# Banded self-attention: the order of four value matmuls and the signal at their end

## The reference

```python
kb, vb = with_prev(kr), with_prev(vr)          # key and value block n-1 and n, side by side
scores = jnp.einsum('bnqhgd,bnkhd->bhgnqk', qb, kb).astype(jnp.float32) * (SWA_HEAD_DIM ** -0.5) + bias
scores = jnp.where(mask, scores, -jnp.inf)
...
probs = jax.nn.softmax(jnp.concatenate([scores, sink], axis=-1), axis=-1)[..., :-1]
out = jnp.einsum('bhgnqk,bnkhd->bnqhgd', probs.astype(v.dtype), vb)
```

## Time and profile before

| | us |
|---|---|
| median of 3 executions (2558.08 to 2558.94) | 2558.24 |
| span of the profiled execution, first to last instruction | 2555.1 |
| PE busy | 2131.7 |
| DVE busy | 1672.5 |
| ACT busy | 1296.7 |
| from the first transpose of unit 0 to the last PV of unit 15 | 126.7 |

### The profile page before, as it was taken

One profiled execution on the slowest core, in us unless ns is written; L12 is line 12 of the kernel. 1 busy time (PEld: TensorE's weight loads), 2 busy tenths in 40 slices (PEclk: granted clock), 3 DMA queues, 4 the chain that ended last, 5 costly groups with the idle time before them and its releaser, 6 DMA issues.

```text
span 2555.1 us, 27563 instructions
## 1 busy us (share of the span) xinstructions
PE 2131.7 (83%) x9450; PEld 1695.3 (66%) x9450; DVE 1672.5 (65%) x1633; ACT 1296.7 (51%) x1302; POOL 653.4 (26%) x419
## 2 busy tenths in 40 slices
PE   4987777995698988739898989898989898989892
PEld 3766666784377865627676767676767676767672
DVE  3344444325533333378888888888888888888886
ACT  3333433224422243117676767676767676767671
POOL 3033333000000000214333333333333333333332
PEclk9988888997799989859999999999999999999996
DMA  5311111230043320139888989898989888989884
GB/s 167 114 33 33 33 33 50 95 104 0 1 117 114 132 83 17 29 136 329 299 320 294 325 293 317 296 323 295 316 295 322 291 314 296 321 297 315 297 306 176
DMA packets 294053, 506.52 MB, mean 198 GB/s; under 512 B 39201, under 2 KB 80177, under 8 KB 293777
## 3 DMA queue, kind: packets, MB, share of 16 engines
q1 hardware_dynamic: 274640, 486.60, 55.0%
q0 software_dynamic: 9504, 16.80, 1.9%
q10 hardware_dynamic: 9856, 2.42, 0.5%
HBM read 502.06 MB, written 24.67 MB: 206 GB/s over the span
## 4 chain that ended last, share of the span: by engine, by line
PE 62%; DVE 25%; issue 5%; ACT 5%; POOL 1%; ACTq 1%; DMA 1%; DVEq 0%; POOLq 0%; SPq 0%
PE bank L1432 18%; PE bank L1433 17%; PE bank L1434 17%; DVE wlo L412 11%; DVE act L1375 3%; PE bank L1514 2%; ACT Ss L820 1%; PE bank L1761 1%; PE bank L1638 1%; PE bank L1630 1%; DVE act L1372 1%; PE bank L1791 1%; DVE aT_lo L1383 1%; DVE res L1413 1%; ACTq L651 1%
## 5 line engine op out<-in xcount | busy, mean ns | idle before, releaser
L412 DVE TENSOR_TENSOR wlo<-raw,whi 128x2048 fp32r<-128x2048 f32 x320 | 857.0, 2695 | 77.7 <-ACT whi L926 76.3
L926 ACT ACTIVATE whi<-raw 128x2048 fp32r<-128x2048 f32 x384 | 715.4, 1908 | 35.8 <-PE bank L1434 35.4
L412 POOL TENSOR_TENSOR wlo<-raw,whi 128x2048 fp32r<-128x2048 f32 x64 | 326.2, 5097 | 395.4 <-PE bank L1434 395.4
L1432 PE MATMUL bank<-whi,xgT_hi 128*128 128x512 f32 x1024 | 426.1, 416 | 1.1
L1433 PE MATMUL bank<-wlo,xgT_hi 128*128 128x512 f32 x1024 | 400.5, 391 | 0.0
L1434 PE MATMUL bank<-whi,xgT_lo 128*128 128x512 f32 x1024 | 400.4, 391 | 0.0
L1432 PE MATMUL bank<-whi,aT_hi 128*128 128x512 f32 x512 | 235.4, 460 | 121.6 <-DVE wlo L412 121.6
L978 DVE TENSOR_TENSOR wlo<-raw,whi 128x2048 fp32r<-128x2048 f32 x58 | 134.5, 2320 | 211.4 <-ACT whi L673 211.3
L1432 PEld LDWEIGHTS bank<-whi,xgT_hi 128*128 128x128 f32 x1024 | 194.0, 189 | 55.1 <-POOL wlo L412 14.2
L1433 PE MATMUL bank<-wlo,aT_hi 128*128 128x512 f32 x512 | 225.3, 440 | 0.0
L1434 PE MATMUL bank<-whi,aT_lo 128*128 128x512 f32 x512 | 223.1, 436 | 0.0
(11 more groups left out here) (288 smaller groups left out, 3363.2 us busy)
## 6 DMA issues: line engine op xcount, KB each, us to landing
raw<-in_w_gate_up_dram SPq DMA_DIRECT2D x256, 1024.0 KB, 5.7
raw<-in_w_down_dram SPq DMA_DIRECT2D x128, 1024.0 KB, 7.2
raw<-in_w_in_dram SPq DMA_DIRECT2D x26, 1024.0 KB, 5.2
yg<-y_d SPq DMA_DIRECT2D x16, 512.0 KB, 8.6
raw<-in_w_in_dram SPq DMA_DIRECT2D x16, 256.0 KB, 4.4
raw<-in_w_branch_a_dram SPq DMA_DIRECT2D x4, 1024.0 KB, 5.1
raw<-in_w_branch_b_dram SPq DMA_DIRECT2D x16, 256.0 KB, 7.9
raw<-in_w_mix_out_dram SPq DMA_DIRECT2D x4, 1024.0 KB, 5.3
```

The lines of the kernel that those rows point to most:

```text
L412: ops.tensor_tensor(m_lo_at[j % M_LO][:], m_raw_at[j % M_RAW][:], m_hi_at[j % M_HI][:].bitcast(F32), ALU.subtract).then_inc(m_lod_p if j i ...
L926: s.activation(m_hi_at[j % M_HI][:], m_raw_at[j % M_RAW][:], ACT.Copy).then_inc(m_hid, 1)
L1432: mm(out_, l_hi, r_hi, start=first, stop=False)
```

## The change

In PV the loop over the key block `s_` becomes the outer one and that over the group e the inner one, so the matmuls alternate between the two column tiles. PE waits for both copies, `PTs0` and `PTs1`, ahead of the first matmul. The last matmul of each column tile signals `bank_full`, where before only the last of all did, and the table counts two for each PV.

```diff
@@ -299,7 +299,7 @@
     for key, b in proj_jobs() + side_jobs():
         if b >= 4 or key[0] in ("pv", "xo", "rt", "rl", "ps", "cn", "tl"):
-            fcount[b] += 1
+            fcount[b] += 2 if key[0] == "pv" else 1
             full_at[key] = fcount[b]
@@ -1633,11 +1633,13 @@
                 opened(pe, key)
                 for e in range(2):
                     after_free(("t", w, e))
-                    kv = 2 * p_ + e
-                    for s_ in sbs:
+                for s_ in sbs:
+                    for e in range(2):
+                        kv = 2 * p_ + e
                         ins = mm(ps[w % 4][64 * e:64 * e + 64, 0:256], vS[:, n - 1 + s_, kv * 64:kv * 64 + 64],
                                  PTs[e][:, s_].rearrange("p i t -> p (i t)"), start=(s_ == sbs[0]), stop=(s_ == 1))
-                done(ins, key)
+                        if s_ == 1:
+                            done(ins, key)
```

## The result

The changed kernel takes 2562.9 us (median of 20 executions, 2559.7 to 2566.9), the kernel before 2558.1 us in as many (2556.6 to 2559.8). The ratio is 1.0020, with a 95% interval of 1.0013 to 1.0027: slower by 4.8 us. The profiled execution has a span of 2562.7 us, where that of before had 2555.1. The changed kernel's profiled execution took 2564.5 us, which is 1.8 above its span and 1.6 above its median. All its executions lie 1.7 to 1.8 us above their spans. So the two profiles differ by 4.8 + 1.6 + 1.2 = 7.6 us.

What follows compares the result with a forecast made beforehand. Bound in attention by two close branches between transposes and exponential, PV with its `o_hi` copy and DVE's; span 2555.1 + 1.1 (release, signal) + 1.2 (clock) = 2557.4, giving a time of 2560.5 us, range 2555.5 to 2563.5.

Steps and rivals of the forecast that it cites:

- PV already overlapped: In PV, the two column tiles already run as independent streams, so the alternating order gains nothing.
- The rival that it would break the overlap: In PV, tiles taking turns: PV needs 3.8 us and ends 1.9 us later, up to 2581 us; chance 0.06.
- The release and the signal: Before PV and the copy to `o_hi`: PV ends 0.09 us later, the second signal adds 0.01 us a unit.
- PV on the chain in ten units: In attention, ten of 16 units pay 0.10 us; with 0.1 for two nearly level ones, +1.1 us.
- the rival of a halved PV: PV's block shrinks by 1.3 us, 4.3 us in all, to 2553.9; chance 0.12 shared with gains by the clock.
- The clock in the stage: In attention, an idle gap of about 0.7 us before PV delays or prevents PE's clock rises: +1.2 us.
- I take a third of the slow end: Clock term: fifteen units all slow would be +3.5 us; a third of that, +1.2 us, was taken.
- The rival of a clock that stays low throughout: In attention, PE's clock never rises: 1.1 + 3.5 = +4.6 us, 2562.8; chance 0.14.
- The clock behind the stage: After attention, no clock effect was forecast; any difference outside the fifteen units' stretch was called not foreseen.

Runs made afterwards that it cites:

- e2: Changed kernel with the alternation and two signals, but PE waits for `PTs1` only ahead of e = 1's first matmul: 2558.4 us, ratio 0.9999.
- e1: Kernel before with only the earlier wait: PE waits for `PTs0` and `PTs1` ahead of the first PV matmul; old order, single signal: 2565.0 us, ratio 1.0024.
- e3: Kernel before with only the second signal: each column tile's last matmul signals, count doubled, order and waits as before: 2558.5 us, ratio 0.9999.
- e7: Changed kernel with one extra 128x128 matmul a unit between transposes and PV: 2561.9 us, ratio 1.0015.
- e4: Changed kernel with two extra 128x128 matmuls a unit between transposes and PV, into unread columns of the bank: 2557.3 us, ratio 0.9998.
- e8: Changed kernel with two extra 128x128 matmuls a unit behind the scores, the gap before PV left open: 2558.7 us, ratio 1.0005.

## Why the prediction was right, and where it was off

**PV already overlapped: right.** `e2` shows it best. With the two signals and a wait for each tile the alternation changes nothing (0.9999), where the rule of the Trainium skill that the prediction cites, that matmuls start in the program's order, would have had it gain. The rival that it would break the overlap fell too: both tiles run together in 2.00 us.

**The release and the signal: right.** Taken at +0.09 us and 0.01 for the second signal, from the rows of the copies; measured 4.76 against 4.65 us in unit 1, +0.11. The traces split it: from the end of the copy to `PTs1` to the start of the copy to `o_hi` unit 1 takes 2.06 us before, 2.16 with the earlier wait alone (`e1`) and 2.17 with the change. So the release is 0.10 and the second signal 0.01. That small price hangs on how far apart the two tiles end. With one signal the copy to `o_hi` starts 0.037 us after PV's last record ends. With two it is 0.037 where the tiles end 0.2 us or more apart (`e2`, `e3`), 0.044 at 0.035 us apart (the change), 0.062 at 0.018 (`e7`) and 0.072 to 0.076 at 0.003 to 0.007 (most units of `e4`). The ends of PE's records are modelled, but the copies' own times go with them: in unit 1 of `e4` the 2.06 us above are 2.20. The Trainium skill gives about 26 ns for each increment (TensorE: Matmul & The Clock Gate, Part 3, The cost: per-tile semaphore tail); by that the twelve units with PV on the chain would have paid some 0.3 us, an estimate. The change paid 7 ns a unit, `e4` up to 39.

**PV on the chain in ten units: now twelve.** All units with n > 0 have it there. That makes 12 x 0.11 = 1.3 us, for a forecast of 1.1. By the prediction's own rows PV was late by 602.04 - 601.69 = 0.35 us in unit 1, not 0.33; only the rival of a halved PV uses it.

**The clock in the stage: right kind, size too small.** The step that failed is "I take a third of the slow end". Fifteen units take 714.20 - 588.61 = 125.59 us now. Of their +3.18 us, 1.2 are by this reckoning the release in eleven units, and the 2.0 left are the clock, for 1.2 forecast. The granted clock of 0.54 says that it hardly rose at all. The rival of a clock that stays low throughout was the better picture. That its 2562.8 is the measured time is luck: it put all 4.6 us into the fifteen units, which show 3.18.

**The clock behind the stage: missing.** The working took the stage alone and said that a difference outside was not foreseen. It came: the gate projection starts at the half clock (+1.27 us) and a restart further on catches the rise later (+1.26 us). In the profiles these three parts add up to 6.2 us, more than the 4.8 of the medians, so they can't be carried over to the medians one by one. The changed kernel's times spread over 7.2 us, those of before over 3.2; that the later restarts fall differently from one execution to the next would explain both, but with one profile for each kernel it isn't shown. The forecast of 2560.5 was 2.4 us short, half of the loss; its range held with 0.6 us to spare.

What stays open: why the stretch behind the memory transposes loses 1.26 us in the change and 1.31 in `e1`, but gains 1.48 in `e8`, which has the hole as well. I can show that the rise comes later in the change, not what fixes the moment.

## What to carry to other kernels

The two column tiles of TensorE overlapped here by themselves, in either order in the program, with a wait for each or one for both. One wait for both operands cost the later tile only 0.1 us, but it opened a gap in front. Where PE is busy in short stretches and its clock goes to and fro between the two levels, a gap of 0.8 us can cost more than the delay that it makes, and part of the bill comes in the next stage. Reckon such a change in granted clock by stage as well as in durations. A few matmuls for nothing, put where PE waits anyway, can earn 0.3%.

## What the runs showed of the hardware

- Two column tiles are independent streams: in the kernel before, a load and a matmul of the second tile started between two of the first (590.66 before 590.78), and the order in the program changed nothing (0.9999).
- The granted clock of the stage went from 0.69 to 0.54 with a hole of 0.78 us in units of 8 to 9 us, back to 0.73 by 0.85 us of matmuls in it. On the kernel before, twelve matmuls in the idle stretch of each unit brought it to 0.97.
- The extra work need not stand in the hole: two matmuls a unit behind the scores brought the clock back to 0.69, with 11.9 us of waits for the copies still there.
- The first weight load of PV, whose list waits for three semaphores, came 0.11 us after the copy that was the last of them to be ready; a load that stood behind a running stream came after 0.05 us.
- Two signals from two tiles to one waiting copy cost 0.035 to 0.039 us more than one when the tiles ended 0.003 to 0.007 us apart, 0.007 at 0.035 us apart and nothing at 0.2 us.
